# Odd layer of a two-layer decoder: value jobs moved behind the queries, attention one unit deeper

## The reference, cut to what matters

```python
h = rms_norm(x)                                  # (512, 1024)
q, kc, vc, ks, vs, kw, vw, gates = split(h @ w_in)   # q 8 heads x 128; each k and v 2 groups x 128
kc, vc = silu(blocks(kc) @ w1) @ w2, silu(blocks(vc) @ v1) @ v2     # 31 compressed keys and values
for branch k, v in (kc, vc), (ks, vs), (kw, vw): # queries and all three kinds of keys are normed
    p = softmax(q @ k.T * scale + bias[distance], causal)
    o += sigmoid(gate[branch]) * (p @ v)
x = x + o @ w_out
x = x + moe(rms_norm(x))                         # 32 experts, top 2
```

## Time and profile before

| | us |
|---|---|
| median of the runs | 1655.53 |
| the profiled execution's own time | 1657.83 |
| its span in the profile | 1655.7 |
| PE busy | 1591.3 (96%) |
| DVE, ACT, POOL busy | 486.9, 359.3, 197.6 |
| odd projection and turns, on PE | from 813.83 to 977.62 |
| odd attention, on PE | from 977.62 to 1099.08 |

### The profile page before, as it was taken

How to read it: one execution, slowest core, us unless ns; L and a number is a source line. 1 busy time by engine, 2 the same in 40 slices (tenths; PEclk the granted TensorE clock), 3 DMA queues, 4 the chain that set the end, 5 groups by cost and what they waited for, 6 DMA issues and landing times.

```text
span 1655.7 us, 21206 instructions
## 1 busy us (share of the span) xinstructions
PE 1591.3 (96%) x8024; PEld 750.4 (45%) x8024; DVE 486.9 (29%) x1254; ACT 359.3 (22%) x839; POOL 197.6 (12%) x298
## 2 busy tenths in 40 slices
PE   7999899999999999999899989999999999999995
PEld 4545574543333333333445457865433333333332
DVE  1485751531111111111412235653611111111114
ACT  2345351311111111011200235642211101111110
POOL 2340220000000000000101012320000000000000
PEclk9999999999999999999999999999999999999998
DMA  7620217289999999999914220033799999999997
GB/s 241 254 102 7 71 37 305 109 342 421 422 421 422 421 422 422 422 423 406 348 20 156 86 55 1 2 159 147 284 422 421 421 422 422 422 422 422 422 421 312
DMA packets 118312, 474.20 MB, mean 286 GB/s; under 512 B 40821, under 2 KB 47221, under 8 KB 68332
## 3 DMA queue, kind: packets, MB, share of 16 engines
q1 hardware_dynamic: 110156, 456.98, 68.9%
q10 hardware_dynamic: 3136, 8.40, 1.3%
q0 software_dynamic: 4960, 8.04, 1.3%
HBM read 454.84 MB, written 26.77 MB: 291 GB/s over the span
## 4 chain that ended last, share of the span: by engine, by line
PE 77%; SPq 12%; DMA 4%; DVE 3%; issue 2%; ACT 1%; POOL 1%; DVEq 0%; ACTq 0%; POOLq 0%
PE bank L1863 19%; SPq L1809 10%; PE bank L1876 9%; PE bank L1480 8%; PE bank L1836 8%; PE bank L551 7%; PE bank L849 6%; PE bank L439 4%; DMA arena<-in_moe_w_up 3%; PE bank L404 3%; PE bank L1851 2%; SPq L1818 2%; PE bank L930 2%; PE bank L421 2%; PE bank L1869 1%
## 5 line engine op out<-in xcount | busy, mean ns | idle before, releaser
L1863 PE MATMUL bank<-arena 128*64 128x512 f32 x2048 | 451.5, 593 | 6.5 <-DMA arena<-in_moe_w_up 6.1
L1863 PEld LDWEIGHTS bank<-arena 128*64 128x64 f32 x2048 | 143.7, 137 | 302.2 <-issue 290.8
L1876 PE MATMUL bank<-arena 128*64 128x512 f32 x1024 | 230.6, 593 | 2.1 <-DVE arena L1969 2.1
L1965 DVE TENSOR_TENSOR arena<-arena,bank 128x256 f32<-128x256 f32 x64 | 27.0, 422 | 637.4 <-ACT arena L1955 637.3
L1882 POOL DMA_INDIRECT y_d<-arena,slot_row x62 | 60.7, 979 | 857.8 <-ACT arena L1960 830.6
L1836 PE MATMUL bank<-arena 128*64 128x512 bf16 x1272 | 160.2, 382 | 0.1
L1480 PE MATMUL bank<-arena 128*128 128x512 f32 x320 | 138.4, 594 | 0.8 <-ACT arena L321 0.8
L1876 PEld LDWEIGHTS bank<-arena 128*64 128x64 f32 x1024 | 71.9, 137 | 124.1 <-issue 110.5
L1955 ACT ACTIVATE arena<-bank 128x256 f32<-128x256 f32 x64 | 24.6, 384 | 410.8 <-PE bank L1863 410.8
L551 PE MATMUL bank<-arena 128*128 128x512 f32 x256 | 111.9, 594 | 0.0
L849 PE MATMUL bank<-arena 128*128 128x512 f32 (+1 forms) x288 | 105.3, 525 | 0.0
(11 more groups left out here) (314 smaller groups left out, 1462.5 us busy)
## 6 DMA issues: line engine op xcount, KB each, us to landing
arena<-in_moe_w_gate SPq DMA_DIRECT2D x128, 1024.0 KB, 20.2
arena<-in_moe_w_up SPq DMA_DIRECT2D x128, 1024.0 KB, 23.3
arena<-in_moe_w_down SPq DMA_DIRECT2D x62, 2048.0 KB, 23.6
arena<-in_even_w_in SPq DMA_DIRECT2D x4, 2048.0 KB, 8.0
y_d<-arena ACTq DMA_DIRECT2D x2, 4096.0 KB, 16.8
arena<-y_d SPq DMA_DIRECT2D x8, 1024.0 KB, 9.2
arena<-bias_row_d SPq DMA_DIRECT2D x2, 3584.0 KB, 11.2
arena<-in_odd_w_in SPq DMA_DIRECT2D x3, 2048.0 KB, 8.2
```

The costliest lines, as they stand in the source:

```text
L1863: mm = nc.tensor.matmul(bank[1][fh * CAP:(fh + 1) * CAP, :], xeT[:, j, half * CAP:(half + 1) * CAP], wgu[u][:, :, n, fh * FH:(fh + 1) * FH ...
L1876: mm = nc.tensor.matmul(bank[3][dh * CAP:(dh + 1) * CAP, :], hidT[:, j, fh * CAP:(fh + 1) * CAP], wd[u][:, n, dh * 512:(dh + 1) * 512], st ...
```

## The change

Three of the four value jobs move to the end, and the queries' and keys' turns are put between jobs. The jobs are now: 0 to 3 compressed inputs, 4 to 7 keys, 8 to 11 first half of the queries, 12 gates, 13 the values of tile 0 of the rows, 14 to 17 second half of the queries, 18 to 20 the values of tiles 1 to 3. The keys of tile i are turned behind job 14+i, the compressed product stands behind the first of these, the first half of the queries is turned behind job 18 and the second behind job 19. The query turns use four banks (4 to 7) where they used two (2 and 3). The chunks of weights are reordered to match: chunk 2 is now one piece, chunk 4 two. The attention (of both layers) is one unit deeper: PE turns unit t-3 and multiplies values of unit t-4; the first turn of the odd attention waits for the last value job's copy.

```diff
+        AHEAD = 3
...
 
             def pe(self, pe):
                 N = len(self.seq)
-                for t in range(N + 3):
+                for t in range(N + AHEAD + 1):
+                    if t == AHEAD and self.values_in:
+                        pe.wait_ge(*self.values_in)
                     u = self.seq[t] if t < N else {}
                     if "m" in u and not (u.get("paired") and u["b"] % 2):
                         self.scores(pe, [u, self.seq[t + 1]] if u.get("paired") else [u])
-                    if 2 <= t < N + 2:
-                        self.turn(pe, self.seq[t - 2])
-                    if t >= 3 and "m" in self.seq[t - 3]:
-                        self.values(pe, self.seq[t - 3])
+                    if AHEAD <= t < N + AHEAD:
+                        self.turn(pe, self.seq[t - AHEAD])
+                    if t > AHEAD and "m" in self.seq[t - AHEAD - 1]:
+                        self.values(pe, self.seq[t - AHEAD - 1])
...
-                    if 2 <= t < N + 2 and self.seq[t - 2]["copy"] == "dve":
-                        self.copy_out(dve, self.seq[t - 2])
-                    if t >= 5 and self.seq[t - 5].get("b") == self.NB - 1:
-                        u = self.seq[t - 5]
+                    if AHEAD <= t < N + AHEAD and self.seq[t - AHEAD]["copy"] == "dve":
+                        self.copy_out(dve, self.seq[t - AHEAD])
+                    if t >= AHEAD + 3 and self.seq[t - AHEAD - 3].get("b") == self.NB - 1:
+                        u = self.seq[t - AHEAD - 3]
                         dve.wait_ge(self.sem("coef"), self.base["m"] + u["m"] + 1)
                         dve.wait_ge(self.sem("pv"), u["a"] + 1)
                         self.finish(self, dve, link, u).then_inc(self.sem("o"), 1)
...
-        OD_CHUNKS = [[(C_OK, 512)], [(C_OK + 512, 256), (C_OK + 1024, 256)], [(C_OK + 768, 256), (C_OK + 1280, 256)],
-                     [(C_GL, 3 * HEADS)], [(0, 512)], [(512, 512)]]
-
-        K_C, K_K, K_V, K_G, K_Q, K_END = 0, 4, 8, 12, 13, 21
-        OD_JOBS = [K_K, K_V, K_G, K_Q, K_Q + 4, K_END]
+        OD_CHUNKS = [[(C_OK, 512)], [(C_OK + 512, 256), (C_OK + 1024, 256)], [(0, 512)],
+                     [(C_GL, 3 * HEADS)], [(C_OK + 768, 256), (C_OK + 1280, 256)], [(512, 512)]]
+
+        K_C, K_K, K_Q0, K_G, K_V0, K_Q1, K_V1, K_END = 0, 4, 8, 12, 13, 14, 18, 21
+        K_VALUES = [K_V0, K_V1, K_V1 + 1, K_V1 + 2]
+        OD_JOBS = [K_K, K_Q0, K_G, K_G + 1, K_END, K_V1]
...
+        def job_bank(n):
+            return bank[(n + 3) % 4]
...
+            sp.wait_ge(S("op_mm"), past("op_mm") + K_G + 1)
             sp.dma_start(o_wo[1], ins["odd_w_out"][0, :, 512:1024].rearrange("(k p) c -> p k c", p=P)).then_inc(S("oo_w1"), 16)
             sp.wait_ge(S("op_mm"), past("op_mm") + K_END)
             sp.dma_start(o_wo[0], ins["odd_w_out"][0, :, 0:512].rearrange("(k p) c -> p k c", p=P)).then_inc(S("oo_w0"), 16)
...
-            for c, first in ((1, K_K), (2, K_V)):
-                pe.wait_ge(S(f"op_w{c}"), past(f"op_w{c}") + 32)
+                job(K_C + j, [(job_bank(j)[:, :], lambda k: ow[0][:, k, j * P:(j + 1) * P], lambda k: hT[:, k, :])])
+            for c, first, loaded in ((1, K_K, 32), (2, K_Q0, 16)):
+                pe.wait_ge(S(f"op_w{c}"), past(f"op_w{c}") + loaded)
                 for i in range(NT):
-                    tokens(first + i, ow[c], i, 512)
+                    tokens(first + i, ow[c], i)
...
+            pe.wait_ge(S("op_w4"), past("op_w4") + 32)
...
+            tokens(K_V0, ow[1], 0)
+            pe.wait_ge(S("hid_c"), past("hid_c") + 2)
+            for q in range(2):
+                mm = nc.tensor.transpose(bank[(7, 5)[q]][:, 0:OG * NC], hid_rows[C_ROWS[q], :],
+                                         ident[C_ROWS[q], C_ROWS[q]])
+            mm.then_inc(S("hid_turned"), 1)
...
             pe.wait_ge(S("op_ev"), past("op_ev") + K_G + 1)
             for i in range(NT):
                 mm = nc.tensor.transpose(bank[6][:, i * P:(i + 1) * P], gT[:, i * P:(i + 1) * P], ident[:])
             mm.then_inc(S("g_turned"), 1)
-            pe.wait_ge(S("hid_cT"), 2)
-
-            for i in range(NT):
+
+            def turn_keys(i):
...
                     n = 2 * i + q
                     if n >= 2:
                         pe.wait_ge(S("ok_out"), past("ok_out") + n - 1)
+                    elif q == 1:
+                        pe.wait_ge(S("hid_cT"), 2)
                     for g in range(OG):
                         mm = nc.tensor.transpose(bank[4 + q][:, g * P:(g + 1) * P], krows[:, q, i, g * OD:(g + 1) * OD], ident[:])
                     mm.then_inc(S("ok_turned"), 1)
-            pe.wait_ge(S("ok_out"), past("ok_out") + 2 * NT)
...
-            for q in range(2):
-                for g in range(OG):
-                    mm = nc.tensor.matmul(bank[4 + q][0:NC, g * P:(g + 1) * P], hidT_c[:, q, g * NC:(g + 1) * NC],
-                                          cw2[:, q, :], start=True, stop=True)
-                mm.then_inc(S("c_rows"), 1)
+
             pe.wait_ge(S("op_w5"), past("op_w5") + 16)
             for i in range(NT):
-                tokens(K_Q + 4 + i, ow[2], i, 512)
-            pe.wait_ge(S("op_ev"), past("op_ev") + K_END)
+                tokens(K_Q1 + i, ow[2], i)
+                turn_keys(i)
+                if i == 0:
+                    pe.wait_ge(S("hid_cT"), 2)
+                    pe.wait_ge(S("gl_sum"), 1)
+                    for q in range(2):
+                        for g in range(OG):
+                            mm = nc.tensor.matmul(bank[6 + q][0:NC, g * P:(g + 1) * P], hidT_c[:, q, g * NC:(g + 1) * NC],
+                                                  cw2[:, q, :], start=True, stop=True)
+                        mm.then_inc(S("c_rows"), 1)
+
...
+            def turn_queries_odd(half):
+                for i in range(NT):
+                    n = NT * half + i
+                    pe.wait_ge(S("oq_n"), past("oq_n") + n + 1)
+                    if n >= 4:
+                        pe.wait_ge(S("oq_out"), past("oq_out") + n - 3)
+                    for j in range(4):
+                        c = (4 * half + j) * P
+                        mm = nc.tensor.transpose(bank[4 + n % 4][:, j * P:(j + 1) * P], rows[:, i, c:c + P], ident[:])
+                    mm.then_inc(S("oq_turned"), 1)
+
+            tokens(K_V1, ow[1], 1)
+            pe.wait_ge(S("kc_raw"), past("kc_raw") + 2)
             pe.wait_ge(S("kc_n"), past("kc_n") + 1)
             for g in range(OG):
                 mm = nc.tensor.transpose(bank[7][:, g * NC:(g + 1) * NC], kc_rows[:, g, :], ident[0:NC, 0:NC])
             mm.then_inc(S("kc_turned"), 1)
...
+            pe.wait_ge(S("ok_out"), past("ok_out") + 2 * NT)
             pe.wait_ge(S("kcT"), past("kcT") + 1)
+            turn_queries_odd(0)
+            tokens(K_V1 + 1, ow[1], 2)
+            turn_queries_odd(1)
+            tokens(K_V1 + 2, ow[1], 3)
             pe.wait_ge(S("oq_out"), past("oq_out") + 2 * NT)
             odd_att.pe(pe)
...
             for j in range(4):
-                ev(K_C + j, cT[:, j // 2, j % 2, :], bank[j][:, :])
...
+                ev(K_C + j, cT[:, j // 2, j % 2, :], job_bank(j)[:, :])
+            for i in range(NT):
+                ev(K_K + i, krows[:, :, i, :], split(job_bank(K_K + i)[:, :], 2, OKV))
+            for i in range(NT):
+                ev_queries(0, i)
...
+            ev(K_G, gT, job_bank(K_G)[:, :])
+            ev_values(0)
+            act.wait_ge(S("hid_turned"), 1)
+            for q in range(2):
+                nc.scalar.activation(hidT_c[:, q, :], bank[(7, 5)[q]][:, 0:OG * NC], ACT.Copy).then_inc(S("hid_cT"), 1)
...
+            act.wait_ge(S("g_turned"), 1)
+            for i in range(NT):
+                ev_queries(1, i)
+                keys_turned(i)
+                if i == 0:
+                    act.wait_ge(S("gl_sum"), 1)
+                    nc.scalar.activation(gl[:], gl[:], ACT.Exp, scale=-1.0).then_inc(S("gl_exp"), 1)
+                    act.wait_ge(S("c_rows"), past("c_rows") + 1)
+                    nc.scalar.activation(kc_rows, split(bank[6][0:NC, 0:OG * OD], OG, OD), ACT.Copy).then_inc(S("kc_raw"), 1)
...
+            ev_values(1)
             act.wait_ge(S("kc_turned"), past("kc_turned") + 1)
             nc.scalar.activation(kcT, split(bank[7][:, 0:OG * NC], OG, NC), ACT.Copy, scale=qk_gain[:, 3:4]).then_inc(S("kcT"), 1)
             act.wait_ge(S("qscale"), past("qscale") + 1)
-            for half in range(2):
-                for i in range(NT):
-                    n = NT * half + i
-                    act.wait_ge(S("oq_turned"), past("oq_turned") + n + 1)
-                    nc.scalar.activation(oqT[:, 4 * half:4 * half + 4, i * P:(i + 1) * P], split(bank[2 + n % 2][:, :], 4, P),
-                                         ACT.Copy, scale=qk_gain[:, 0:1]).then_inc(S("oq_out"), 1)
+            queries_turned(0)
+            ev_values(2)
+            queries_turned(1)
+            ev_values(3)
...
```

(4 more changed lines are left out.)

84 lines of the change are left out of this document (28 added, 56 removed).

## The result

The changed kernel takes 1644.84 us, median of 5 runs (1643.35 to 1646.34), beside 1655.53 (1654.09 to 1660.22) for the kernel before: ratio 0.993, 95% interval 0.9918 to 0.9942, 10.7 us less. Run again later it took 1645.08 (6 runs) beside 1657.38 (17 runs): ratio 0.9932 (0.9919 to 0.9946). The forecast was 1643.0, range 1639.5 to 1648, and the time is inside it.

A forecast was written before the change was run, and what follows sets the result against it. PE was taken as the bound, winnable only where it idles or runs slowly: -11.5 us before the steady attention and -1.0 in the odd attention, -12.5 in all, took 1655.53 to 1643.0; range 1639.5 to 1648.

The forecast's parts named there:

- Key turns: Odd layer, 16 key turns in groups of four behind long jobs: 1.76 us where they took 4.57, -2.81.
- compressed keys' wait: Before the first query turns, PE idles about 0.8 us for ACT's copy, replacing a wait of 0.69: +0.1.
- query turns: Odd layer, 32 turns up to the first score: 3.52 us for 9.60, with scaling and copies covered by jobs: -6.08.
- Opening: Start of the odd attention: 2.81 us for 5.49 at full clock and without waits, -2.68; bounds 0 to -3.2.
- the other half is the clock: Opening of the odd attention: work sums to 2.81 of 5.49 us; the rest was put down to granted clock 0.50.
- Odd attention one unit deeper: Odd attention: tile 0 loop +1.4, its exponential waits -1.2, tile 1 -0.7, `odd_turn` places -0.5; sum -1.0 us.
- rival A: Both attentions: the deeper order takes nearly all idle time, -17.9 us in all, so 1637.6; chance 0.10.
- Even attention: Even layer's attention one unit deeper: less cover for DVE's copy against three small ACT waits; 0, between -1.2 and +1.6 us.
- Transfers and experts: Reordered weight chunks land in time, cost 0; the expert stream moves with the attention's end, so the whole gain arrives.
- B: Odd attention: opening stays slow, tile 0's loop grows by 1.4 with no waits gone; 1648.1 us, chance 0.14.
- C: Clock falls at the compressed keys' wait or in tile 0 of the attention; 1655 us, no change; chance 0.02.
- D: Slower: every c values product waits for DVE's copy in all tiles, 0.5 a head over 32 heads; 1660 us, chance 0.03.

The follow-up runs named there:

- two fillers: The kernel before, with two identity matmuls added in front of TensorE's wait for the scaled second half of the queries: 1655.57 us, ratio 0.9995.
- order-only kernel: The changed kernel with both attentions back at a distance of two units, keeping only the new job order: 1648.13 us, ratio 0.994 to the kernel before.

## Why the prediction was right, and where it was off

- **Key turns, -2.81; compressed keys' wait, +0.1; query turns, -6.08.** Sum -8.79, measured -8.83. The places were those named: no idle time at the key groups, one wait of 0.70 (said: 0.8) before the first query turns, none for L1718. Undone one at a time, the hidden key and query turns cost 2.23 and 2.02, and the wait for the compressed keys, when it was taken away, gave 0.70. The rest of the query turns' term was the wait for VectorE's scaling, the two banks, and 0.6 to 1.0 of clock in the last turns (163.79 and 164.16 in the two profiles of before, beside 163.16 with two fillers), which I had counted in the 9.60 without saying that it was clock.
- **Opening, -2.68.** Measured -2.64, but of two parts, told apart by the order-only kernel: 1.9 by the clock (5.49 to 3.60), 0.75 by the depth (3.60 to 2.85). So "the other half is the clock" was too much: at distance two the opening takes 3.60 to 3.68 at full clock, with a wait of 0.53 for the first exponential, and my sum of 2.81, which has no wait in it, is reached only by the deeper order. The low stretch runs from 975.0 to 981.8: it begins 1.6 behind the end of the pause and ends 1.3 before the opening does. And the clock's part was taken from one profile that had the long low stretch. Where the short one comes, the whole of it lies in the query turns and the opening costs 3.68. The order's gain is 10.7 against the one profile and 9.3 against the other (167.84 to 158.56); the timed order-only kernel shows 8.9.
- **Odd attention one unit deeper, -1.0.** Mis-sized: -4.2, inside my bounds (-5.15 to +2.8) but towards their edge, and what rival A was about, though only for this attention. From the first scores of one width to those of the next, tiles 3, 2, 1 and 0 take 35.31, 33.24, 25.56 and 21.86 before and 34.49, 31.87, 24.16 and 21.88 after. In tile 0 the sum came out near the forecast, about nothing, or 0.7 less at most (its stretch after holds the turns and the product of one unit more, 0.66 at tile 3's size), but its parts did not: the waits for exponentials, 1.2, are gone as forecast, while the waits for DVE's copies went from 2.1 to 2.2 in the list of waits, so the 1.4 by which the loop was to grow never came. Tiles 3 and 2 I had taken for full, on their 0.76 of idle time, and they gave 2.2; tile 1 gave 1.4, not 0.7. Before, PE waited seven times in these three tiles for DVE's copy of c, 1.6 in all by the list of waits, after not once. The list and the busy time hide the rest, because a late start that falls within the tail of the matmul before it counts as busy. Read from start to start, against the usual step of each width (0.11 for 128 columns, 0.43 for 512), the values products lose 2.4 less after than before, and the turns behind a c score 1.1 less (six of them start 0.1 to 0.3 late before, none after).
- **Even attention, 0.** The step that failed: +2.2 to +2.5, above the bound of 1.6. I counted the cover of DVE's copy and overlooked that in this attention scores come in pairs, so that an odd distance puts two turns together. That the time came out within 1.8 of the forecast is in part luck: this error (2.2) and that of the odd attention (3.2) have opposite signs.
- **Transfers and experts, 0.** Right: job 14 waits for nothing, and the stretch behind the odd attention takes 556.62 before and 557.20 after.
- **Rivals.** A falls for the kernel: the time is far from its 1637.6, and the even attention grew. B and C fall: the clock is 1.00 in the opening and in tile 0 in every profile of the new order. D falls: no wait for the copy in tiles 3 and 2. The argument against C was weaker than it looked, though: elsewhere in this kernel the clock does fall behind waits of 1.0 (see the end). The rule of the Trainium skill weighed there ("TensorE: Matmul & The Clock Gate", section "A second HAM failure mode: psum-queue depth-cycling") isn't borne out by these eight profiles, in which tile 0 idles in pieces of up to 0.64 at 1.00.
- **Median and profile.** The profiled pair differs by 14.5 and the medians by 10.7 and 12.3. 1.4 of it is the low stretch that before alone had in layer 0, and up to 1.4 the longer one in its opening. The profiled execution of the changed kernel was also the fastest of its five. That the slower ones had more low stretches is likely but not shown, since only one of them has a trace.

Of the 55 timed runs of the kernel before beside the experiments, the four with a mean granted clock of 0.993 took 1654.5 to 1655.3, the four at 0.988 or less 1660.2 to 1663.0. So a part of this kernel's spread goes with the number of low stretches that an execution catches; not all, for those at 0.991 alone lie between 1654.6 and 1659.5.

## What to carry to other kernels

Price a wait by the work behind it too: the pause of 2.56 cost itself and 1.0 to 2.4 more in slow turns and scores. In the traces a few idle matmuls that fit in such a pause (1.9 into 2.6, 4.6 into 4.9 in two pieces) give that back, while matmuls that don't fit take it away again; in the times of the first of these the gain is not clear of the scatter. Put small turns one group at a time behind a long job, so that another engine's copies are off the path (2.2 for the keys, 2.0 for the queries). And set the distance of a software pipeline for each loop by its own grouping: one unit more gave 5.0 in the odd layer and took 2.4 in the even one, where two units are issued as a pair.
